# Attention outputs normalised by one VectorE operation a head, gates multiplied on GpSimd, forget term added with the mask

## What is computed

```python
def _dense_causal(q, k, v, scale, cum=None):      # MLA and FOX, in 128-query blocks
    s = einsum('bqhd,bkhd->bhqk', q_blk, k) * scale
    if cum is not None:                           # FOX: the forget term
        s = s + c_q[..., :, None] - cum_t[:, :, None, :]
    s = where(k_pos[None, :] <= q_pos[:, None], s, NEG_INF)
    p = softmax(s, axis=-1)
    return einsum('bhqk,bkhd->bqhd', p, v)

def _fox_branch(x, w_in, b_f, w_out):
    ...
    log_f = log_sigmoid(f_logit + b_f)            # (B, S, 16 heads)
    cum = cumsum(log_f, axis=1)
    o = _dense_causal(q, k, v, HEAD_DIM ** -0.5, cum).reshape(B, S, W)
    return (o * silu(gate)) @ w_out               # MLA and SWA end in the same way
```

## Time and profile before

| what | value |
|---|---|
| runs | 1794.48, 1796.54, 1799.9 us (median 1796.54) |
| profiled execution, its own time | 1797.55 us |
| profiled execution, span from first to last instruction | 1795.8 us |
| TensorE busy | 1645.5 us, 92% |
| VectorE busy | 1199.2 us, 67% |
| ScalarE busy | 864.6 us, 48% |
| GpSimd busy | 57.7 us, 3% |
| chain that ended last, share on TensorE | 76% |
| granted TensorE clock, mean | 0.931 of full speed |

### The profile page before, as it was taken

One profiled execution on the slowest core, in us unless ns is written; L12 is line 12 of the kernel. 1 busy time (PEld: TensorE's weight loads), 2 busy tenths in 40 slices (PEclk: granted clock), 3 DMA queues, 4 the chain that ended last, 5 costly groups with the idle time before them and its releaser, 6 DMA issues.

```text
span 1795.8 us, 31252 instructions
## 1 busy us (share of the span) xinstructions
PE 1645.5 (92%) x10734; PEld 1410.9 (79%) x10734; DVE 1199.2 (67%) x2585; ACT 864.6 (48%) x1380; POOL 57.7 (3%) x88
## 2 busy tenths in 40 slices
PE   7888998898888888699879999989999999999996
PEld 6766967796567767587669999989999777778885
DVE  4775565554336675654665899978878899975554
ACT  4653354444224663344334666656565344444543
POOL 1200000100001020000000000000000000000000
PEclk9998998998558998899889999999999999999998
DMA  7542553453214554453345455544444444456562
GB/s 260 193 148 93 182 174 111 162 176 128 72 59 165 182 165 171 168 194 106 118 141 165 151 172 183 188 148 152 162 153 157 147 164 164 164 202 194 190 195 83
DMA packets 76677, 282.99 MB, mean 158 GB/s; under 512 B 9328, under 2 KB 9344, under 8 KB 75328
## 3 DMA queue, kind: packets, MB, share of 16 engines
q1 hardware_dynamic: 73280, 266.95, 44.9%
q0 software_dynamic: 3328, 15.14, 2.3%
HBM read 279.94 MB, written 2.12 MB: 157 GB/s over the span
## 4 chain that ended last, share of the span: by engine, by line
PE 76%; DVE 15%; ACT 4%; issue 3%; DMA 1%; DVEq 0%; ACTq 0%; POOLq 0%
PE banks L585 21%; PE banks L586 20%; PE banks L587 20%; DVE w_lo L1225 4%; PE banks L914 3%; PE banks L674 2%; PE banks L627 2%; PE banks L709 2%; PE banks L649 1%; PE banks L721 1%; PE banks L720 1%; ACT scratch L1038 1%; PE banks L678 1%; PE banks L719 1%; DVE arena L1370 1%
## 5 line engine op out<-in xcount | busy, mean ns | idle before, releaser
L1225 DVE TENSOR_TENSOR w_lo<-raw,w_hi 128x1024 fp32r<-128x1024 f32 x456 | 559.3, 1230 | 366.1 <-ACT w_hi L972 363.2
L972 ACT ACTIVATE w_hi<-raw 128x1024 fp32r<-128x1024 f32 x456 | 482.5, 1059 | 562.6 <-PE banks L587 537.7
L585 PE MATMUL banks<-w_hi,xT_hi 128*128 128x512 f32 (+2 forms) x1140 | 456.8, 401 | 15.8 <-DVE xT_lo L1257 9.7
L586 PE MATMUL banks<-w_lo,xT_hi 128*128 128x512 f32 (+2 forms) x1140 | 447.3, 392 | 0.0
L587 PE MATMUL banks<-w_hi,xT_lo 128*128 128x512 f32 (+2 forms) x1140 | 446.7, 392 | 0.0
L585 PE MATMUL banks<-xT_hi,w_hi 128*128 128x256 f32 x1360 | 393.2, 289 | 2.1 <-DVE arena L1277 1.2
L586 PE MATMUL banks<-xT_lo,w_hi 128*128 128x256 f32 x1360 | 387.0, 285 | 0.0
L587 PE MATMUL banks<-xT_hi,w_lo 128*128 128x256 f32 x1360 | 386.6, 284 | 0.0
L585 PEld LDWEIGHTS banks<-w_hi,xT_hi 128*128 128x128 f32 x1140 | 220.1, 193 | 62.9 <-issue 14.4
L585 PEld LDWEIGHTS banks<-xT_hi,w_hi 128*128 128x128 f32 x1360 | 262.8, 193 | 3.6 <-issue 3.6
L586 PEld LDWEIGHTS banks<-xT_lo,w_hi 128*128 128x128 f32 x1360 | 263.2, 194 | 0.0
(11 more groups left out here) (189 smaller groups left out, 1512.4 us busy)
## 6 DMA issues: line engine op xcount, KB each, us to landing
raw<-stream SPq DMA_DIRECT2D x504, 512.0 KB, 3.6
arena<-ln_in POOLq DMA_DIRECT2D x4, 1024.0 KB, 4.9
arena<-mod_rows POOLq DMA_DIRECT2D x2, 1536.0 KB, 7.6
arena<-g_in POOLq DMA_DIRECT2D x3, 512.0 KB, 7.4
arena<-x_in SPq DMA_DIRECT2D x1, 1024.0 KB, 5.1
arena<-bands_in POOLq DMA_DIRECT2D x1, 1024.0 KB, 5.4
arena<-keys_in POOLq DMA_DIRECT2D x1, 1024.0 KB, 5.9
x_spill<-arena POOLq DMA_DIRECT2D x1, 1024.0 KB, 4.9
```

What stands on the lines that cost most here:

```text
L585: pe.matmul(out, stationary[0], moving[0], start=first, stop=False, **k)
L586: pe.matmul(out, stationary[0], moving[1], start=False, stop=False, **k)
L972: act.activation(w_hi[:, s], half_raw(s), ACT.Copy).then_inc(piece_hi, 1)
L1225: dve.tensor_tensor(w_lo[:, s], half_raw(s), w_hi[:, s].bitcast(F32), ALU.subtract).then_inc(piece_lo, 1)
```

## The change

Three things are done.

- `normalise` takes one VectorE `tensor_tensor` for both query blocks of a head: the 128x(2x64) output in bank 7 times the reciprocals, spread over the 64 columns. It no longer reads the gate. This holds for all 72 heads, moba's 8 among them.
- GpSimd multiplies the gates in place, in each of the four layers in five groups of heads (0-3, 4-7, 8-11, 12-14, 15), each when its heads' outputs are taken. TensorE's first transposes of the outputs wait for two groups, the second ones for all five.
- `aug`, `head_rows` and the second score matmuls go. VectorE writes the negated cumulative sums and signals `f_ready`. GpSimd stores them to HBM (16 KB), loads them back three times spread over all partitions (each 16 runs of 512 bytes to each of 128 partitions, so 1024 KB), and adds the causal mask to two of the three parts (128 x 16 x 128 elements each). `scale_mask` reads head h's part of that `forget_mask` in place of the causal mask. Only the key side of the term is kept: the query side is constant along a row, and the softmax takes it away.

```diff
+GATE_GROUPS = ((0, 4), (4, 8), (8, 12), (12, 15), (15, 16))
...
+        forget_mask = cut(11264, HEADS, 3, P)
...
+            def gate_heads(l):
+                L = layers[l]
+                if L["kind"] == "mla":
+                    pool.wait_ge(gate_silu, l // 3 + 1)
+                    o, gate = mla["o"], mla["h"][:, :, MLA_GATE:]
+                else:
+                    wait_put(pool, L["gate"])
+                    o, gate = attn["o"], attn["gate"]
+                for lo, hi in GATE_GROUPS:
+                    pool.wait_ge(out_taken, HEADS * l + hi)
+                    mine = o[:, :, lo * HD:hi * HD]
+                    pool.tensor_tensor(mine, mine, gate[:, :, lo * HD:hi * HD], ALU.mult).then_inc(gated_heads, 1)
+                pool.wait_ge(gated_heads, len(GATE_GROUPS) * (l + 1))
...
+                if layers[l]["kind"] == "fox":
+                    sums = x_spill[0:2].rearrange("a b n -> (a b n)")
+                    pool.wait_ge(f_ready, 1)
+                    pool.dma_start(sums.rearrange("(h t) -> h t", t=S), forget[:, 0]).then_inc(f_stored, 16)
+                    pool.wait_ge(f_stored, 16)
+                    spread = sums.rearrange("(h t) -> h t", t=S).partition_broadcast(P)
+                    for part, block in ((0, 0), (1, 0), (2, 1)):
+                        load(forget_mask[:, :, part], spread[:, :, block * P:(block + 1) * P], f_spread)
+                    pool.wait_ge(f_spread, 48)
+                    own = const("causal")[:, 0:P].unsqueeze(1).broadcast_to([P, HEADS, P])
+                    for part in (0, 2):
+                        pool.tensor_tensor(forget_mask[:, :, part], forget_mask[:, :, part], own, ALU.add).then_inc(f_masked, 1)
...
+                gate_heads(l)
                 if l == DEPTH - 1:
-                    pool.wait_ge(out_taken, DEPTH * HEADS)
...
-                if fox:
-                    pe.wait_ge(aug_ready, h + 1)
                 for cols, qb, n in (((0, P), 0, P), ((P, 3 * P), 1, 2 * P)):
                     mm = pe.matmul(bank[:, cols[0]:cols[1]], qh[:, qb * P:(qb + 1) * P], kh[:, 0:n],
-                                   start=(qb == 0), stop=not fox, skip_group_check=True)
-                    if fox:
-                        r = HD * (h % 2)
-                        mm = pe.matmul(bank[:, cols[0]:cols[1]], attn["aug"][r:r + 48, h % 2, qb * P:(qb + 1) * P],
-                                       aug[r:r + 48, 1, 0:n], start=False, stop=True, skip_group_check=True)
+                                   start=(qb == 0), stop=True, skip_group_check=True)
...
-                for u in L["oT"]:
+                for u, groups in zip(L["oT"], (2, len(GATE_GROUPS))):
+                    pe.wait_ge(gated_heads, len(GATE_GROUPS) * l + groups)
                     turn(u, o)
...
-                    if kind == "fox" and h + 1 < heads:
-                        head_rows(h + 1)
...
+                        added = forget_mask[:, h].rearrange("p c n -> p (c n)") if kind == "fox" else const("causal")
+                        ins = dve.scalar_tensor_tensor(out=s_sb[:, g % 2], in0=raw_scores, scalar=scale, in1=added,
...
-                    for b in range(B):
-                        src = banks[:, 7, b * HD:(b + 1) * HD]
-                        if gate is None:
-                            ins = dve.tensor_scalar(o[:, b, h * HD:(h + 1) * HD], src, r[:, b:b + 1], None, ALU.mult)
-                        else:
-                            ins = dve.scalar_tensor_tensor(out=o[:, b, h * HD:(h + 1) * HD], in0=src, scalar=r[:, b:b + 1],
-                                                           in1=gate[:, b, h * HD:(h + 1) * HD], op0=ALU.mult, op1=ALU.mult)
+                    ins = dve.tensor_tensor(o[:, :, h * HD:(h + 1) * HD], banks[:, 7, 0:B * HD].rearrange("p (b d) -> p b d", b=B),
+                                            r.unsqueeze(2).broadcast_to([P, B, HD]), ALU.mult)
                     ins.then_inc(out_taken, 1)
 
                 if kind == "fox":
-                    head_rows(0)
+                    dve.wait_ge(f_masked, 2)
                 for h in range(2):
                     scale_mask(h)
...
-                    dve.wait_ge(aug_loaded, 16)
-                    for r in (0, HD):
-                        note(dve.tensor_scalar(aug[r + 32:r + 32 + HEADS, 0], t, 8.0, None, ALU.mult))
-                        note(dve.tensor_scalar(aug[r:r + HEADS, 1], t, -8.0, None, ALU.mult))
-                    settle()
+                    dve.tensor_scalar(z, t, -1.0, None, ALU.mult).then_inc(f_ready, 1)
```

More of the change, by code:

```diff
@@ L237, in build @@
         attn = dict(qT=cut(0, KD, S), kT=cut(2048, KD, S), v=cut(4096, B, D), gate=cut(6144, B, D),
-                    o=cut(8192, B, D), aug=cut(13056, 2, S))
-        aug = cut(13568, 2, S)
+                    o=cut(8192, B, D))
+        forget_mask = cut(11264, HEADS, 3, P)
         forget = cut(10240, 3, S)[0:HEADS]
@@ L391, in build @@
         probs_ready, probsT_full, probsT_ready = sem("probs_ready"), sem("probsT_full"), sem("probsT_ready")
[L392 to L393 removed]
+        out_full, out_taken, gated_heads = sem("out_full"), sem("out_taken"), sem("gated_heads")
+        f_abs, f_exp, f_ready = sem("f_abs"), sem("f_exp"), sem("f_ready")
+        f_stored, f_spread, f_masked = sem("f_stored"), sem("f_spread"), sem("f_masked")
         c_loaded, mod_stored, mod_loaded = sem("c_loaded"), sem("mod_stored"), sem("mod_loaded")
@@ L538, in _ @@
                     load(ln_gb.rearrange("p a n -> p (a n)"), rows(ln_in[l + 1]), ln_loaded)
-                if l == 0:
-                    load(aug.rearrange("p a n -> p (a n)"), aug_in, aug_loaded)
                 if l == DEPTH - 2:
@@ L662, in ada_rows, with scores @@
                         mm.then_inc(unit_full, 1)
-            def scores(h, q, k, fox=False):
+            def scores(h, q, k):
                 g = heads_done[0] + h
@@ L698, in project_half, with attention @@
                     drop_piece(mm)
-            def attention(heads, q, k, v, fox=False, ada=0, late=(), beside=()):
+            def attention(heads, q, k, v, ada=0, late=(), beside=()):
                 g0 = heads_done[0]
@@ L730, in attention @@
                     if i != 1 and max(i + 1, 2) < heads:
-                        scores(max(i + 1, 2), q, k, fox)
+                        scores(max(i + 1, 2), q, k)
                     if ada and i == 5:
@@ L810, in _ @@
                     keys = lambda h: attn["kT"][HD * (h % 2):HD * (h % 2 + 1), h // 2]
-                    first_scores(queries, keys, True)
+                    first_scores(queries, keys)
                     project(L["gate"][1])
-                    attention(HEADS, queries, keys, lambda h, b: attn["v"][:, b, HD * h:HD * (h + 1)], fox=True,
+                    attention(HEADS, queries, keys, lambda h, b: attn["v"][:, b, HD * h:HD * (h + 1)],
                               ada=ADA_CHUNKS, late=L["late"])
@@ L1315, in ada_unit, with attention @@
                                          op1=ALU.add).then_inc(ada_summed, 1)
-            def attention(heads, kind, scale, o, gate, ada=None, between=None, gate_ready=None, last_split=None,
+            def attention(heads, kind, scale, o, ada=None, between=None, gate_ready=None, last_split=None,
                           beside=()):
@@ L1467, in _ @@
                 split_ahead(L["xT"][-1].pieces_done)
-                def gates_landed():
-                    wait_put(dve, L["gate"])
                 if L["kind"] == "mla":
@@ L1512, in _ @@
                         evacuate(u)
-                    attention(HEADS, "swa", HD ** -0.5, attn["o"], attn["gate"], l,
-                              lambda: split_ahead(L["gate"][1].pieces_done - 1), gates_landed,
+                    attention(HEADS, "swa", HD ** -0.5, attn["o"], l,
+                              lambda: split_ahead(L["gate"][1].pieces_done - 1), None,
                               lambda: split_ahead(L["gate"][1].pieces_done))
@@ L1566, in mix @@
                 split_ahead(M["mixT"][0].pieces_done)
-            attention(MOBA_HEADS, "moba", HD ** -0.5, moba["o"], None, between=mix,
+            attention(MOBA_HEADS, "moba", HD ** -0.5, moba["o"], between=mix,
                       gate_ready=lambda: wait_put(dve, M["gates"]), beside=M["pool"])
```

22 lines of the change are left out of this document (6 added, 16 removed).

## The result

| | before | changed |
|---|---|---|
| median of the runs, us | 1797.34 (1794.48 to 1799.9, 4 runs) | 1743.83 (1732.2 to 1751.09, 4 runs) |
| profiled execution, its span, us | 1797.55, 1795.8 | 1751.09, 1749.3 |
| ratio of the times | | 0.9697, 95% interval 0.9633 to 0.976 |

The median is 53.5 us lower (by the interval 43 to 66) and 0.2 us from the forecast of 1744. The four runs spread over 19 us, those of the kernel before over 5; the profile is of the slowest of the four. Five more runs of the same kernel, taken later as `e0_after_again`, gave 1746.9 (1739.0 to 1753.11), ratio 0.9711 [0.9683, 0.9739].

A forecast was written before the change was run, and what follows sets the result against it. It took FOX's loop to be bound by a circle of TensorE and VectorE waits at a low clock. Terms 53.5 + 3.5 + 3.6 - 7 = 53.6 us off 1797.55 gave 1744, main case 1732 to 1757.

The forecast's parts named there:

- three signs that the prediction named for being wrong: Loads landing after 430, clock staying at 0.5 in FOX's loop, or a `w_lo` of several microseconds before a waiting matmul.
- Circle gone, SWA as template: FOX, first scores to loop's end: TensorE and VectorE stop waiting on each other; priced by SWA's stretch, gain 53.5 us.
- the sink: SWA's extra exponential and two small VectorE operations a head, absent in new FOX: a further gain of 3.5 us.
- Normalisation, 3.6 us: Loops over heads: one operation of 0.33 us replaces two in 0.47, gaining 0.9 us a loop, 3.6 for four.
- Gates on GpSimd, nothing: Loops over heads: GpSimd's gate multiplications are hidden, and the last groups end before TensorE's transposes need them; cost nothing.
- When the mask is there: Ahead of FOX's loop: store, transfer of 25 us and additions of 5.8 us each leave the mask ready at 423.7.
- the latest harmless time: Ahead of FOX's loop: the mask must be there by 417 or so for `ada_chunk` 0's weights to land in time.
- What a late mask costs, 7 us, one for each microsecond: Ahead of FOX's loop: every microsecond the mask comes after 417 costs one; the cost is 7 us.
- clock stays low: Rival, chance 0.08: FOX's loop starts at 1.2 GHz after a wait and stays there; 31 us lost, 1775 us.
- VectorE held up by the additions, 0.06 and 5.9 us: Rival, chance 0.06: GpSimd's two additions let no `w_lo` between them and stall TensorE by 5.9 us; 1750.
- the late mask: Rival, chance 0.12: small packets make the mask's transfer ahead of FOX's loop take 40 to 70 us; 1757 to 1787.
- slower end: Rival, chance 0.06: small packets cost what large ones do, the transfer takes up to 96 us; 1815 us.

The follow-up runs named there:

- e1: Changed kernel without the mask building (no store, loads, additions or wait; FOX takes the causal mask): 1729.01 us, ratio 0.9631 to the kernel before.
- e4: Kernel before with only the one-operation normalisation and the gates on GpSimd, forget term still in the matmuls: 1788.41 us, ratio 0.9943.
- e5: Changed kernel with the old two-operation normalisation, gate on VectorE, none on GpSimd: 1759.48 us, ratio 0.9791 to the kernel before.
- e13: Changed kernel without mask building, TensorE made to wait for a GpSimd memset ahead of FOX's `ada_chunk` 0: 1747.24 us, ratio 0.9714.
- e6: Changed kernel plus seven filler matmuls of 128x512 on TensorE ahead of `ada_chunk` 0 in FOX: 1737.11 us, ratio 0.9685.
- e11: Changed kernel with GpSimd's two additions of 2048 elements split into eight of 512: 1749.65 us, ratio 0.9731.
- e12: Changed kernel with VectorE's three `w_lo` ahead of FOX's loop put before the mask wait and first two `scale_mask`s: 1738.44 us, ratio 0.9670.
- e7: Changed kernel with the forget sums scanned after the first key unit, not the second: 1730.94 us, ratio 0.9639.
- e10: Changed kernel with scan after the first key unit, eight short additions, and one 2 MB load in 1 KB runs: 1733.07 us, ratio 0.9638.

## Why the prediction was right, and where its terms were not

The total held, 53.5 us measured and 53.6 forecast, and so did the main mechanism, the circle that goes. But that the two agree to 0.1 us is luck: the saving without the mask's cost was some 5 us larger than forecast, the mask's cost 5 to 7 us larger too, and the same kernel gave medians of 1743.8 and 1746.9 in two sets of runs. And the profiled execution did not look as forecast: FOX's loop took 61.6 us at a clock of 0.64, not 42 to 45 near 0.9. Of the three signs that the prediction named for being wrong, the loads after 430 did not come (they landed by 406.83), but the clock stayed at 0.50 for more than half of the loop, and a `w_lo` of 5.63 us did stand before a waiting matmul.

- **Circle gone, SWA as template.** Right. The FOX loop without the mask's cost is 40.45 us at 0.99 (e1), and the stretch from `first_scores` to its end 459.06 - 405.42 = 53.6 us, where the template less the sink gave 60.2 - 3.5 = 56.7. The whole saving without that cost was forecast at 60.6 us and is 66 (1 - 0.9631 of 1795.41, interval 62 to 70); 3.1 of the difference lie in this stretch. The template itself is less firm than it looked: SWA's loop takes 42.5 to 48.6 us in the traces of these runs with one and the same code for it, at clocks of 0.99 to 0.79.
- **Normalisation, 3.6 us.** Mis-sized. The operation takes 0.292 us, not 0.33, so 0.18 a head is saved, not 0.14, and each MLA loop is 1.4 to 1.7 us shorter, not 0.9; if the saved time is all there is to it, some 9 of the 16 heads are on the path, not 6.6. That makes 3.3 us in the two MLA loops of e4; FOX gained nothing, and the 1.4 of SWA's loop are less than it varies by. The time of e4 fell by 10. In its profiled execution most of the rest lies behind the loops, in the three output projections (5.5 us, at a clock of 0.94 and 0.95 for 0.86). Whether the change brings that clock is not shown: in the changed kernel, with the same normalisation, two of these three stretches take 29.7 us at 0.84 and only the third 27.4. Nor do e4 and e5 separate the operation from the move of the gates. Both stay open.
- **Gates on GpSimd, nothing.** Right. The last groups take 1.00 and 0.45 us, and the first transposes start at 486.61, while the last group runs, 0.45 us behind the last normalisation.
- **When the mask is there.** Forecast 423.7. `first_scores` came 2.2 us earlier in this execution (410.03 for 412.26), so that is 421.5, and the latest harmless time 414.8. It was there at 416.98: transfer 22.7 us for 25, additions 4.60 and 5.6 for 5.8 each. So in the prediction's own terms it was late by 2.2 us, not by 7. The first, by itself in the timeline:

```profile
406.83 4.60 POOL L548 TENSOR_TENSOR arena<-arena 128x2048 f32<-128x2048 f32 x1 [19.15 <-DMA arena<-x_spill]
```

  The 4497 ns of the Trainium skill (GPSIMD Engine Reference, "Elementwise — side-by-side cycle accounting") agree with these 4.60 us better than the 5.8 scaled up from 256 elements.
- **What a late mask costs, 7 us, one for each microsecond.** This is the step that failed. The chain behind it was the one forecast: late `scale_mask`, late `w_lo` of the output's first pieces (5.8 us), late `ada_chunk` 0, TensorE idle (4.2 us). But a mask 2.2 us late should have cost 2.2 us by that rule, and the price was 12 to 14. The held-up `w_lo` added their part to the delay (see the next point), and with them `ada_chunk` 0 was done 6.8 us later than in e1, by chance about the 7 forecast. The rest is the clock, which came down in the pause and stayed at 1.2 GHz for 37 us; e13 shows that with the pause alone, and e6, with about the same delay and without the low clock, is 8 us above e1. The rival "clock stays low" was right about the place, and wrong in that it would last: the loop recovered by itself. It had 0.08 as another outcome; it belonged into the term as what each such pause costs.
- **VectorE held up by the additions, 0.06 and 5.9 us.** It happened, and ahead of the wait for the mask: `w_lo` of 4.26 and 5.63 us against 1.21. It stalled TensorE by 1.49 us in the gate unit, not by 5.9, since each addition let one `w_lo` in. The reason given against it, that the second gate unit's pieces would mostly be split by then, did not hold: when the additions began, one of the four was. The rule of the Trainium skill (SBUF — State Buffer, "Who interferes with whom") agrees with the trace: the `w_lo` at 412.44 lasts until 418.07, 1.1 us past the end of the second addition. The two causes overlap, but not wholly: VectorE came to the first `scale_mask` 2.1 us after the mask was there, and without the hold-up it could have started at 416.98. e11 and e12 each take one of them away and still show a pause, of 4.9 and 3.0 us.
- **Many small packets.** Neither the late mask nor the slower end came: the 3.15 MB were 816 packets in the trace.

## What to carry to other kernels

Where a loop runs near the full clock, price a stall of TensorE ahead of it not by its own microseconds but by these and the stretch at the lower clock behind it: here 5 us idle cost 15 (e13), though 2.4 us within a projection did not bring the clock down for the loop (e7). Before wide elementwise work goes to GpSimd, look at what VectorE does in that time, and put it where neither the held-up operations nor the waits behind them are on the path. And if two causes cover the same time, take both away together: neither by itself won anything clear of the noise here (e11, e12), and moving the scan by one unit won 16 us (e7). A last thing is worth taking along: two profiled executions can differ by some us in a loop that the change leaves alone, at another clock, so a gain of 1 or 2 us read from one pair of traces needs a second pair.

## What the runs showed that was not expected

- After a pause of 3.0 us (e12), 4.2 us (changed kernel), 4.9 us (e11) or 5.3 us (e13) ahead of the loop TensorE ran at 1.2 GHz for 29 to 40 us although it was busy almost without a gap; in e7, around a wait of 2.43 us inside a projection, the clock was 0.83 over ten microseconds (405 to 415) and 1.00 until the loop. What makes the one pause cost so much more than the other was not tried.
- The changed kernel spreads over 19 and 14 us in its two sets of runs and e12 over 22, while e1 spreads over 7 and e10 over 5. The low clock alone does not make the spread: e13 has it and spreads over 4.
- SWA's loop, whose code is the same in eleven of the kernels traced, takes 42.5 us (once), 44.8 to 45.1 or 48.4 to 48.6, at a clock of 0.99, 0.88 or 0.79, and the output projection behind a loop 27.4 or 29.3 to 29.8 us at 0.94 or 0.85. What decides between them was not looked for.
- A GpSimd addition of 2048 elements takes 4.6 to 5.6 us; eight of 512 take 12.96 us in place of 10.15 (e11), but a `w_lo` beside them is held by 0.8 us only, not by 3 to 4.4.
- A transfer of 3.15 MB in runs of 512 bytes, beside a stream with 46% of the engines, took 22.7 us in 816 packets; 2 MB in runs twice as long took 13.1 us (e10).
